# A transformer block pair on one core: latent attention's queries and keys computed transposed

## The reference

```
p = h @ w_in[l]
u_f, z_f, cq, ckv, k_r, z_a = jnp.split(p, split_pts, axis=-1)
...
q = (_rmsnorm(cq, q_norm[l]) @ w_q_b[l]).reshape(B, S, N_HEADS, QK_HEAD_DIM)
q_nope, q_rope = q[..., :QK_NOPE_DIM], _apply_rope(q[..., QK_NOPE_DIM:], cos_q, sin_q)
kv = (_rmsnorm(ckv, kv_norm[l]) @ w_kv_b[l]).reshape(B, S, N_HEADS, QK_NOPE_DIM + V_HEAD_DIM)
k_nope, v = kv[..., :QK_NOPE_DIM], kv[..., QK_NOPE_DIM:]
k_rope = _apply_rope(k_r, cos, sin)
y_a = _mla_attention(q_nope, q_rope, k_nope, k_rope, v) * jax.nn.silu(z_a)
```

## Time and profile before

| | |
|---|---|
| median of 3 runs | 2184.77 us (2184.72 to 2185.58) |
| the profiled execution, span from first to last instruction | 2182.5 us, core 0 alone |
| PE busy | 2170.6 us, 99% |
| PEld busy (overlaps PE) | 1800.3 us, 82% |
| DVE, ACT busy | 1522.8 us (70%), 1110.2 us (51%) |
| mean granted clock of PE | 0.999 |
| moved by DMA | 502.87 MB, 230 GB/s over the span |

### The profile page before, as it was taken

How to read it: one execution, slowest core, us unless ns; L and a number is a source line. 1 busy time by engine, 2 the same in 40 slices (tenths; PEclk the granted TensorE clock), 3 DMA queues, 4 the chain that set the end, 5 groups by cost and what they waited for, 6 DMA issues and landing times.

```text
span 2182.5 us, 27829 instructions
## 1 busy us (share of the span) xinstructions
PE 2170.6 (99%) x10870; PEld 1800.3 (82%) x10870; DVE 1522.8 (70%) x2026; ACT 1110.2 (51%) x1521; POOL 47.1 (2%) x66
## 2 busy tenths in 40 slices
PE   9999999999999999999999999999999999999999
PEld 7888887888888888888888888887888887888887
DVE  6675479778867777777777778767465577555566
ACT  6676466444446444444443444566465455446452
POOL 0000000100000000000000000000000000000000
PEclk9999999999999999999999999999999999999999
DMA  9544655598877888988999988574565573655563
GB/s 333 164 146 145 196 180 174 173 391 298 277 283 225 301 305 300 312 299 307 304 302 311 305 303 303 181 244 120 148 190 152 161 253 116 173 167 158 160 231 127
DMA packets 243220, 502.87 MB, mean 230 GB/s; under 512 B 17024, under 2 KB 25456, under 8 KB 241936
## 3 DMA queue, kind: packets, MB, share of 16 engines
q1 hardware_dynamic: 239792, 486.20, 68.4%
q0 software_dynamic: 3296, 14.88, 2.0%
HBM read 498.89 MB, written 2.12 MB: 230 GB/s over the span
## 4 chain that ended last, share of the span: by engine, by line
PE 93%; DVE 2%; ACT 2%; DMA 1%; issue 1%; SPq 0%; POOL 0%; DVEq 0%; ACTq 0%
PE bank L959 90%; PE bank L962 3%; ACT arena L1396 1%; DVE wl L2007 1%; DMA raw<-in_w_in 1%; DMA arena<-in_w_in 1%; DMA raw<-in_w_ple_gate 0%; ACT wh L1396 0%; DVE hl L2007 0%; DVE arena L2010 0%; ACT ah L1396 0%; DVE arena L2015 0%; DVE arena L2014 0%; DVE al L2007 0%; SPq L754 0%
## 5 line engine op out<-in xcount | busy, mean ns | idle before, releaser
L1396 ACT ACTIVATE wh<-raw 128x1024 fp32r<-128x1024 f32 (+2 forms) x500 | 520.9, 1043 | 652.6 <-PE bank L959 600.6
L2007 DVE TENSOR_TENSOR wl<-raw,wh 128x1024 fp32r<-128x1024 f32 (+2 forms) x500 | 599.4, 1201 | 341.2 <-ACT wh L1396 339.5
L959 PE MATMUL bank<-wh,hh 128*128 128x512 f32 (+1 forms) x1568 | 617.0, 394 | 2.4 <-DVE wl L2007 1.2
L959 PE MATMUL bank<-wh,hl 128*128 128x512 f32 (+1 forms) x1568 | 605.0, 387 | 0.0
L959 PE MATMUL bank<-wl,hh 128*128 128x512 f32 (+1 forms) x1568 | 604.0, 386 | 0.0
L959 PE MATMUL bank<-wh,ah 128*128 128x512 f32 (+1 forms) x1168 | 456.1, 391 | 0.9 <-ACT ah L1396 0.6
L959 PE MATMUL bank<-wh,al 128*128 128x512 f32 (+1 forms) x1168 | 450.9, 387 | 0.0
L959 PE MATMUL bank<-wl,ah 128*128 128x512 f32 (+1 forms) x1168 | 450.1, 386 | 0.0
L959 PEld LDWEIGHTS bank<-wh,hh 128*128 128x128 f32 x1568 | 294.8, 188 | 62.2 <-issue 3.5
L959 PEld LDWEIGHTS bank<-wh,hl 128*128 128x128 f32 x1568 | 294.3, 188 | 60.0
L959 PEld LDWEIGHTS bank<-wl,hh 128*128 128x128 f32 x1568 | 294.8, 188 | 55.4
(11 more groups left out here) (136 smaller groups left out, 1354.6 us busy)
## 6 DMA issues: line engine op xcount, KB each, us to landing
raw<-in_w_in SPq DMA_DIRECT2D x245, 512.0 KB, 3.8
arena<-in_w_ada SPq DMA_DIRECT2D x148, 384.0 KB, 4.7
arena<-in_w_gate_up SPq DMA_DIRECT2D x97, 512.0 KB, 4.5
raw<-in_w_ada SPq DMA_DIRECT2D x108, 384.0 KB, 4.8
raw<-in_w_out SPq DMA_DIRECT2D x80, 512.0 KB, 5.0
raw<-in_w_gate_up SPq DMA_DIRECT2D x79, 512.0 KB, 4.5
raw<-in_w_down SPq DMA_DIRECT2D x45, 512.0 KB, 5.2
arena<-in_w_down SPq DMA_DIRECT2D x43, 512.0 KB, 5.2
```

The lines of the kernel that those rows point to most:

```text
L959: return i.matmul(o, l, x, start=start, stop=stop, skip_group_check=False)
L1396: return i.activation(o, x, fn, scale=scale, **k)
L2007: return i.tensor_tensor(o, a, b, op)
```

## The change

The columns of `w_q_b` and `w_kv_b` are reordered on the host, so that all plain query columns stand together, then all rotary ones; all plain key columns, then all values. The blocks of a layer are now zf 0, qr (512 columns: the rotary parts of all 8 heads, 2 units), qn 0 (4 heads' plain queries), kn 0 (4 heads' plain keys, 1 unit), vb 0 (4 heads' values, 1 unit), zf 1, qn 1, kn 1, vb 1, za 0, za 1. Blocks qn and kn are `turned`: 128 by 128 of the weights sit in the array and the 256 tokens of the left operand stream past (`bank<-ah,wh`, 256 columns), so the result comes out with the head's columns on the partitions, as QN and KN are needed. A unit of them is 24 such matmuls; qn has its two units in two halves of 12 matmuls, that is in four slots. ACT copies the results to QN and KN without a scale. So the factors go elsewhere: RK is applied to the latent keys and values before they are transposed (`ckv` now waits for it on ACT, and PE's transposes come two slots later), and RQ times the score scale is RS, which replaces the constant in the exponential and in the maximum. The stage qr copies 512 columns, DVE rotates all 8 heads in one go for each half of the tokens, PE turns them in two groups of four. `mla` begins 6 slots after vb 0.

```diff
             add(f"zf{l}", z, w, 0, 16, 1024 + 512 * z, 512, x)
-            for n in (2 * z, 2 * z + 1):
-                add(f"qb{l}", n, f"w_q_b_2@{l}", 0, 4, 384 * n, 384, y, 4)
-                add(f"kvb{l}", n, f"w_kv_b_2@{l}", 0, 2, 512 * n, 512, y, 6)
+            if z == 0:
+                add(f"qr{l}", 0, f"w_q_b_2@{l}", 0, 4, 1024, 512, y, 4)
+            add(f"qn{l}", z, f"w_q_b_2@{l}", 0, 4, 512 * z, 512, y, 4, turned=True, split=2)
+            add(f"kn{l}", z, f"w_kv_b_2@{l}", 0, 2, 512 * z, 512, y, 6, turned=True)
+            add(f"vb{l}", z, f"w_kv_b_2@{l}", 0, 2, 1024 + 512 * z, 512, y, 6)
...
-            start(done(f"kvb{l}", 1) + 8, "mla", l, z)
+            start(done(f"vb{l}", 0) + 6, "mla", l, z)
...
+                if bl.turned:
+
+                    for h in [2 * k + m for m in ms for k in range(2)]:
+                        for q in range(2):
+                            o, ks = acc[h // 2][:, h % 2 * 256:h % 2 * 256 + 256], slice(q * nw + h * P, q * nw + (h + 1) * P)
+                            mm(o, wh[:, ks], hi[:, q, :], first and q == 0, False)
+                            mm(o, wl[:, ks], hi[:, q, :], False, False)
+                            x = mm(o, wh[:, ks], lo[:, q, :], False, last and q == 1)
...
+            def qr(l):
+                yield from range(4)
+                e.wait_ge(*S.v_qr.at(l, 1))
+                for b in range(2):
+                    four(bank(("qr", l, b), S.a_qr, l, b), QV[:, :, 256 * b:256 * b + 256]).then_inc(*S.p_qr.up(l, b))
+                    yield
...
+            def turned(name, o, l, n):
+
+                z = ended(f"{name}{l}", n)
+                e.wait_ge(*S.p_four.at(l, "o", 3))
+                for k in range(2):
+                    x = copy(o[:, 4 * n + 2 * k:4 * n + 2 * k + 2, :].rearrange("p h t -> p (h t)"), acc(z, k))
                 x.then_inc(*S.a_ev.up(z))
...
-                        x = f(PB[z][:, m, :], ps[:, m, :], ACTF.Exp, scale=SCL, bias=nm[:, m:m + 1], accum=sm[:, m:m + 1])
+                        x = f(PB[z][:, m, :], ps[:, m, :], ACTF.Exp, scale=RS[:, m:m + 1], bias=nm[:, m:m + 1], accum=sm[:, m:m + 1])
...
+            def qr(l):
+                yield
+                e.wait_ge(*S.a_ev.at(INDEX[f"qr{l}", 0]))
+                e.wait_ge(*S.p_kr.at(l))
+                ts(RS, RQ, SCL, None, ALU.mult).then_inc(*S.v_rs.up(l))
+                for m in range(2):
+                    v, a, b = (t[:, m, :].rearrange("p (h z n) -> p h z n", h=8, z=2) for t in (QV, QA, QB))
+                    sn = ROPE[:, 1, 0, m, :].unsqueeze(1).to_broadcast([P, 8, 32])
+                    cs = ROPE[:, 1, 1, m, :].unsqueeze(1).to_broadcast([P, 16, 32])
+                    tt(a.rearrange("p h z n -> p (h z) n"), v.rearrange("p h z n -> p (h z) n"), cs, ALU.mult)
+                    tt(b[:, :, 0, :], v[:, :, 1, :], sn, ALU.mult)
+                    then(tt(b[:, :, 1, :], v[:, :, 0, :], sn, ALU.mult), S.v_qr, l, m, "m")
+                    tt(v[:, :, 0, :], a[:, :, 0, :], b[:, :, 0, :], ALU.subtract)
+                    tt(v[:, :, 1, :], a[:, :, 1, :], b[:, :, 1, :], ALU.add).then_inc(*S.v_qr.up(l, m))
+                    yield
```

More of the change, by code:

```diff
@@ L94 @@
     last: int = 0
+    turned: bool = False
 def plan():
@@ L194, in most @@
     for b in BLK:
-        if b.split and b.half < t <= b.last:
+        if b.split and not b.turned and b.half < t <= b.last:
             return b.g0 + b.nk // 2 + min(2, (t - b.half) // 2)
@@ L496, in timetable @@
         start(done(f"ckv{l}"), "ckv", l)
-        for j in range(4):
-            start(done(f"qb{l}", j), "qb", l, j)
-            start(done(f"kvb{l}", j), "kvb", l, j)
+        start(done(f"qr{l}"), "qr", l)
         for z in range(2):
-            start(done(f"kvb{l}", 1) + 8, "mla", l, z)
-        start(done(f"kvb{l}", 3) + 4, "gate_row", l)
+            start(done(f"qn{l}", z), "qn", l, z)
+            start(done(f"kn{l}", z), "kn", l, z)
+            start(done(f"vb{l}", z), "vb", l, z)
+        for z in range(2):
+            start(done(f"vb{l}", 0) + 6, "mla", l, z)
+        start(done(f"vb{l}", 1) + 4, "gate_row", l)
         start(done(f"za{l}", 1) + 4, "ln_rows", l)
@@ L1874, in ckv @@
                 split(f"Y4{l}", 6, [COLS[:, c:c + 1], COLS[:, c + 1:c + 2]])
-                yield from range(3)
+                yield
                 e.wait_ge(*S.p_kr.at(l))
@@ L1905, in za @@
                     yield
[L1907 to L1913, removed]
-                for m in range(2):
-                    x = copy(TQ2[j % 2][:, m, :], acc(z, m, 384), scale=RQ[:, m:m + 1])
+            def qr(l):
+                z = ended(f"qr{l}")
+                e.wait_ge(*S.p_op.at(f"Y4{l}", 5))
+                for m in range(2):
+                    x = copy(QV[:, m, :], acc(z, m))
+                x.then_inc(*S.a_ev.up(z))
+                yield from range(4)
+                for b in range(2):
+                    e.wait_ge(*S.p_qr.at(l, b))
+                    copy(QR[:, 2 * b:2 * b + 2, :].rearrange("p j t -> p (j t)"), BANK[bank_of["qr", l, b]][:, :]).then_inc(*S.a_qr.up(l, b))
+                    yield
@@ L1916, in qb, with vb @@
+            def vb(l, n):
+                z = ended(f"vb{l}", n)
+                for m in range(2):
+                    x = copy(VN[:, m, 512 * n:512 * n + 512], acc(z, m))
                 x.then_inc(*S.a_ev.up(z))
                 yield
[L1918 to L1940, removed]
@@ L2612, in ckv @@
             def ckv(l):
-                e.wait_ge(*S.a_ev.at(INDEX[f"ckv{l}", 0]))
+                e.wait_ge(*S.a_sq.at("ckv", l, 1))
                 e.wait_ge(*S.g_cq.at(l))
@@ L2636, in ckv @@
                 x.then_inc(*S.v_ckv.up(l, "r"))
+                yield
+                c = COL[f"kv{l}"]
+                split(f"Y4{l}", 6, [COLS[:, c:c + 1], COLS[:, c + 1:c + 2]])
             def zf(l, n):
```

100 lines of the change are left out of this document (38 added, 62 removed).

## The result

The changed kernel takes 2190.39 us (median of 12 runs, 2189.28 to 2193.07) against 2185.01 (12 runs, 2183.88 to 2186.43) for the kernel before on the same chip: ratio 1.0025, 95% interval 1.0017 to 1.0034. It is slower by 0.25% (interval 0.17% to 0.34%), just outside the 0.2% that the prediction called no change, and inside its range. The profiled spans are 2187.5 and 2182.5. A profile is one execution: the twelve runs of the changed kernel had spans of 2187.5 to 2191.2 us, and the profiled one is among the shortest.

The account below looks back on a forecast made before the run. The prediction took PE, busy 99% of the span, to bound the kernel. Per layer, -3.6 + 0.65 - 0.14 + 1.7 + 2.7 = 1.3 us, so 2184.77 becomes 2187.4 us, with a range of 2180.0 to 2193.5.

Parts of the forecast that it names:

- Transposes: On PE, 40 transposes a layer become 8; at 0.1125 us each, 3.6 us a layer go.
- Products: On PE, same columns streamed but 48 more matmuls a layer, 0.12 us each at 256 columns: 0.65 us more a layer.
- the rival that the weight loads set the pace: In turned blocks, 256-column products start 0.146 us apart instead of 0.12: 5.0 us above forecast, 2192.4; chance 0.12.
- Place C: At ckv's transposes, PE's 0.14 us wait for ACT goes and nothing takes its place.
- Place A: Ahead of the first qr transposes, PE waits 1.7 us a layer for DVE's rotation.
- Place B: At the start of za 0, PE waits 2.7 us a layer for ACT's kn 1 copies behind table load and exponentials.
- A third pause: Sign of being wrong: PE shows another uncounted pause besides the forecast 1.7 us before qr's transposes and 2.7 before za 0.
- The clock: Rival: PE's granted clock falls in the za 0 waits, 3.4 us more, 2190.8; with the qr waits too 2194.2; chance 0.13.
- the clock of 1.00 behind both pauses: Sign of being right: PE's granted clock stays 1.00 after the waits at qr's transposes and at za 0.
- The sum: All terms together: 1.3 us a layer more, 2.6 for two; span 2182.5 becomes 2185.1, median 2187.4.
- the slower rivals: Weight loads pacing the 256-column products (2192.4, chance 0.12) and the clock falling in the waits (2190.8 or 2194.2, chance 0.13).
- The drain of the Trainium skill: At za 0's start, a drain of about 1.38 us added to the table load's 1.28; the whole would be 2190.1.

Follow-up runs that it names:

- e6_pad: Changed kernel with mla and qr's transposes and copies each two slots later, plus 64 unread transposes where PE does not wait; 2185.21 us, 1.0000 of before.
- e4_const: Changed kernel with the exponentials scaled by a constant instead of the per-token column RS (result differs); 2187.82 us, 1.0015 of before.
- e3_both: Changed kernel with mla starting two slots later and qr's transposes and copies two slots later; 2176.97 us, 0.9963 of before.
- e1: Changed kernel with only the attention stage mla starting two slots later; 2180.73 us, 0.9979 of before.
- e2: Changed kernel with only qr's transposes on PE and their copies on ACT two slots later; 2187.87 us, 1.0012 of before.
- e8: Changed kernel with qr's transposes and copies two slots later and the exponentials scaled by a constant (result differs); 2185.65 us, 1.0002 of before.
- e5: Changed kernel with only the attention stage mla starting one slot later; 2187.83 us, 1.0012 of before.

## Why the prediction was right or wrong

- **Transposes, -3.6 a layer: right.** e6_pad measures 7.0 to 7.4 for 64, against 7.2.
- **Products, +0.65: right at 256 columns.** 0.119 us, against 0.12 forecast from the line through 320 and 384 columns; the rival that the weight loads set the pace is out. With the turn-over from transposes, which the sum left out at both widths, the term measures 0.5.
- **Place C, the wait for ckv gone: right**; its transposes (1604.99) start 0.23 behind the product ahead, without a wait.
- **Place A, +1.7: right.** 1.74 in both layers.
- **Place B, +2.7: the mechanism was right, the term too small.** It measured 3.2. The price of an exponential was taken from rows of before, where its scale was a constant; the change itself, in the line of its diff that replaces SCL by RS, makes each longer by 0.1 us. Four stand ahead of the copies, and e4_const gives 0.37 of the 0.5 back. The other 0.13 is the table load, which starts 1.08 behind `high` (1680.31 and 1681.39), where the sum took the 0.95 that lie between `high` and a copy.
- **A wait that was not in the list: +0.45** at the first pair's transposes, from the same lengthening (0.38 of it, by e4_const). The prediction looked at three places where the change moves instructions, and not at the places where an instruction that it lengthens ends last. A third pause that it had not counted was one of its own signs of being wrong; this one is small beside the two, and they are as laid out.
- **The clock.** Forecast as a rival with 0.13; it came at one of the two pauses at B and cost 1.6 us, so the clock of 1.00 behind both pauses, which it named as a sign, held at three of the four.
- **The sum.** Forecast +2.6, spans +5.0, of which 4.6 lie between the shared starts. 1.0 from B, 0.1 from A, 0.9 from the first pair and 1.6 from the clock are 3.6 more than forecast; against them stand 1.6 that the kernel gained beyond the count (1.7 by e3_both, where most of it is laid out). So the forecast came as near as it did partly because terms that were missing on both sides cancelled. That 2190.39 lies beside the 2190.8 of the rival of the clock is chance: it priced two falls, and there was one, with longer exponentials in place of the other.
- **The verdict.** "No measurable change" at +0.12%, held with 0.63, became +0.25%, measured as slower, for which it gave 0.27; the range held because it was wide enough for the slower rivals. The main point, that the 6 us which leave PE's list come back as two waits, is shown by e1, e2 and e3: with both waits gone the gain is there. The drain of the Trainium skill (page "ScalarE: Activation LUTs", section "What ACT_TABLE_LOAD costs"), by which B would have been 4.1, does not show: the load starts 0.02 behind the end of `high`, and the first exponential 1.29 behind the start of the load. That the whole came near the 2190.1 which that drain would have given is chance too.

What stays open: when a pause at B makes the clock fall. Behind the eight pauses of 2.8 to 3.2 us at B (after, e2, e4, e8, two layers each) it fell six times, in the changed kernel in the second layer only and in e4_const in the first only. Behind the pauses of 1.7 at A (after, e1, e4, e5) and behind those of e5_mla7 it never fell. Why one pause of 3.2 is followed by a fall and an equal one is not, these runs don't tell. Each count is of one profiled execution, and executions of one kernel differ: the mean granted clock of the twelve runs of the changed kernel lay between 0.995 and 0.998, and their longer spans go with the lower clocks.

## What to carry to other kernels

When a change takes work from the engine that sets the time, the waits for the others come up at once: go through every place where it meets them, with the queue ahead of the instruction that it waits for, and move the start of the stage in question by a slot or two before judging the change. Here two such numbers turned a loss of 0.25% into a gain of 0.37%. Price each instruction in the form that it has after the change, an operand that turns from a constant into a column included.

## What the runs showed of the hardware

- An activation of 128 by 256 with its scale from a column lasts 0.56 us and starts 0.545 behind the one ahead; with a constant 0.47 and 0.45.
- A pause of TensorE of about 3 us, with dense products on both sides, was followed by a fall of the granted clock to the lower level in six of eight cases: mostly 3.4 us long, in one case twice that. The two that can be set beside an equal pause without a fall (in the changed kernel and in e4_const) cost 1.6 us each. A kernel with one pause less can so be hardly faster: e2_qr6 lost 2.4 us more to the clock, of the 3.5 that A gave.
- The fall at the layers' border lasted 3.4 us in seven of the ten profiles and 6.8 in three, and both lengths came in kernels without a pause ahead of it (e3_both, e6_pad). The longer one cost 0.7 to 0.8 us more than the shorter, at a place where PE waits in part.
- Products of 256 columns in this type start 0.119 us apart, each with its own weight load. (The shown length of such a load, 0.19, is no bound on the distance.)
